# Input projections of two mixing stages: float32 products, or three passes of rounded parts split on chip

## What is computed

```python
def token_mix(x, w_in, w_out, ...):
    h = x @ w_in
    (nq, kc, vc, ks, vs, kw, vw, gl, u, gq, gk, gv, ga, gr) = jnp.split(h, split_pts, axis=-1)
    gates = jax.nn.sigmoid(gl).reshape(B, S, NSA_HEADS, 3)
    o_a = nsa_mixer(nq, kv(kc), kv(vc), kv(ks), kv(vs), kv(kw), kv(vw), gates, ...)
    o_b = pool_mixer(u, pool_w, pool_scale)
    o_c = gla_mixer(gq, gk, gv, ga, gr, gla_wa2, gla_ba, gla_norm_g)
    return jnp.concatenate([o_a, o_b, o_c], axis=-1) @ w_out
```

## Time and profile before

| | |
|---|---|
| median of three runs | 2523.66 us |
| the profiled execution | 2522.78 us |
| its span | 2521.0 us |
| granted TensorE clock, mean | 0.973 |
| stage mix0, first product to first L1485 | 220.1 to 284.8 us |
| stage mix1, first product | 766.5 us |
| last products of mix0 (L1423) | until 366.3 us |

### The profile page before, as it was taken

One profiled execution on the slowest core, in us unless ns is written; L12 is line 12 of the kernel. 1 busy time (PEld: TensorE's weight loads), 2 busy tenths in 40 slices (PEclk: granted clock), 3 DMA queues, 4 the chain that ended last, 5 costly groups with the idle time before them and its releaser, 6 DMA issues.

```text
span 2521.0 us, 32805 instructions
## 1 busy us (share of the span) xinstructions
PE 2393.3 (95%) x12825; PEld 1937.4 (77%) x12825; DVE 1778.3 (71%) x2016; ACT 1259.1 (50%) x1345; POOL 148.5 (6%) x175
## 2 busy tenths in 40 slices
PE   7999999999999999989998997889999999999996
PEld 6878858887878768779846885667788888887885
DVE  5773357858763458758454566868889889899897
ACT  4332334334332434344424436737777777777774
POOL 0000000001000000000010003500000000000000
PEclk9999999999999999999999997889999999999998
DMA  9667248757757358644215553138999999999994
GB/s 324 242 248 183 65 150 274 279 182 268 254 201 170 101 185 282 218 176 167 101 67 197 178 175 110 68 142 289 353 354 355 369 334 359 364 354 345 361 350 190
DMA packets 304844, 591.48 MB, mean 235 GB/s; under 512 B 61583, under 2 KB 97109, under 8 KB 304605
## 3 DMA queue, kind: packets, MB, share of 16 engines
q1 hardware_dynamic: 285954, 521.09, 59.0%
q0 software_dynamic: 18352, 68.70, 8.0%
q10 hardware_dynamic: 428, 0.15, 0.0%
HBM read 587.79 MB, written 2.11 MB: 234 GB/s over the span
## 4 chain that ended last, share of the span: by engine, by line
PE 86%; DVE 8%; ACT 3%; issue 2%; DMA 0%; DVEq 0%; SPq 0%; ACTq 0%
PE psum L891 20%; PE psum L893 19%; PE psum L892 19%; PE psum L1361 3%; PE psum L924 3%; PE psum L1368 2%; PE psum L1423 2%; DVE ring_r L1093 2%; PE psum L2084 2%; PE psum L1014 2%; PE psum L2817 2%; PE psum L1981 1%; PE psum L1986 1%; PE psum L1982 1%; DVE arena L3000 1%
## 5 line engine op out<-in xcount | busy, mean ns | idle before, releaser
L1093 DVE TENSOR_TENSOR ring_r<-ring,ring_r 128x2048 fp32r<-128x2048 f32 x286 | 653.3, 2289 | 261.4 <-ACT ring_r L1087 260.8
L1087 ACT CAST ring_r<-ring 128x2048 fp32r<-128x2048 f32 x286 | 546.1, 1911 | 492.8 <-PE psum L893 403.9
L893 PE MATMUL psum<-ring_r,arena_r 128*128 128x512 f32 (+1 forms) x1560 | 596.9, 383 | 0.0
L891 PE MATMUL psum<-ring_r,arena_r 128*128 128x512 f32 (+1 forms) x1016 | 398.6, 392 | 23.1 <-DVE arena_r L1165 11.1
L892 PE MATMUL psum<-ring_r,arena_r 128*128 128x512 f32 (+1 forms) x1016 | 391.2, 385 | 0.0
L1093 DVE TENSOR_TENSOR ring_r<-ring,tail_r 128x2048 fp32r<-128x2048 f32 x143 | 327.3, 2289 | 83.1 <-ACT tail_r L1087 81.8
L1087 ACT CAST tail_r<-ring 128x2048 fp32r<-128x2048 f32 x143 | 273.3, 1911 | 139.4 <-PE psum L893 137.7
L893 PEld LDWEIGHTS psum<-ring_r,arena_r 128*128 128x128 f32 x1560 | 294.5, 189 | 58.0
L893 PE MATMUL psum<-ring_r,z_r 128*128 128x512 f32 (+1 forms) x840 | 311.2, 370 | 0.0
L891 PEld LDWEIGHTS psum<-ring_r,arena_r 128*128 128x128 f32 x1016 | 192.2, 189 | 75.7 <-DVE ring_r L1093 22.7
L892 PEld LDWEIGHTS psum<-ring_r,arena_r 128*128 128x128 f32 x1016 | 192.6, 190 | 35.1
(11 more groups left out here) (467 smaller groups left out, 3239.3 us busy)
## 6 DMA issues: line engine op xcount, KB each, us to landing
ring<-in_moe_w SPq DMA_DIRECT2D x264, 1024.0 KB, 6.7
arena<-in_ada_w POOLq DMA_DIRECT2D x48, 1024.0 KB, 9.1
ring<-in_ffn_wg SPq DMA_DIRECT2D x44, 1024.0 KB, 7.3
ring<-in_ffn_wu SPq DMA_DIRECT2D x44, 1024.0 KB, 7.1
ring<-in_ffn_wd SPq DMA_DIRECT2D x44, 1024.0 KB, 7.0
ring<-in_ffn_w SPq DMA_DIRECT2D x33, 1024.0 KB, 5.4
ring<-in_mlstm_w_in SPq DMA_DIRECT2D x8, 2048.0 KB, 8.3
ring<-in_mlstm_w_out SPq DMA_DIRECT2D x4, 2048.0 KB, 8.9
```

The source lines that it names most:

```text
L891: pe.matmul(dst, lhs_low, rhs, start=start, stop=False)
L893: return pe.matmul(dst, lhs, rhs_low, start=False, stop=stop)
L1087: act.copy(upper[i % UPPERS], place(PN[r.key, i])).then_inc(upper_ready, 1)
L1093: dve.tensor_tensor(low, raw, upper[i % UPPERS], ALU.subtract).then_inc(lower_ready, 1)
```

## The change

Two tables are new: nine pieces of the panels, and the PE event after which each piece's buffer is free. Every piece is split on chip. `mix_high_act` (ACT) waits for the panels of the piece and for its buffer, and writes the rounded high part to one of three buffers (two in a part of the arena that the attention uses later, one in `tail`). `mix_low_dve` (DVE) waits for that and writes the rest over the raw piece. Ahead of a mixing stage ACT's copies of x go to `xh`, rounded, and `mix_split_x_dve` writes the rest to `xT_r`. `features` and `tokens` wait for the piece's low part and make three float32r passes for each float32 matmul of before; in piece 0 the pass over x's rest waits for it. PE's order is changed, and with it two of the events that free a panel (panel 0: gqk in place of gv, panel 1: ga in place of gr).

```diff
-PANEL_END = ("gv", "gr", "q1", "kcvc", "vwgl", "u")
+PANEL_END = ("gqk", "ga", "q1", "kcvc", "vwgl", "u")
+
+PIECES = [[(0, 256, 256)], [(1, 0, 272)], [(0, 0, 256)], [(2, 0, 256)], [(2, 256, 256)], [(3, 256, 128), (4, 128, 128)],
+          [(3, 0, 256)], [(4, 0, 128), (4, 256, 152)], [(5, 0, 256)]]
+PIECE_END = ("gv", "ga", "gqk", "q0", "q1", "kskw", "kcvc", "vwgl", "u")
...
+    def mix_high_act(act, l, c):
+        for i, first, w in PIECES[c]:
+            act.wait_ge(*landed(PN["mix", l, "in", i]))
+        if c < 2:
+            act.wait_ge(mod_done, (2 * l + 1) * NC)
+        elif c == 2:
+            for b in PN["mix", l, "upper"].before:
+                act.wait_ge(*b)
+        else:
+            act.wait_ge(*mixP.after(PIECE_END[c - 3], l))
+        for high, raw in zip(upper_pieces(c), raw_pieces(l, c)):
+            ins = act.copy(high, raw)
+        ins.then_inc(*mixH.inc(f"hi{c}", l))
+
+    def mix_low_dve(dve, l, c):
+        dve.wait_ge(*mixH.after(f"hi{c}", l))
+        for high, raw, low in zip(upper_pieces(c), raw_pieces(l, c), raw_pieces(l, c, ring_r)):
+            ins = dve.tensor_tensor(low, raw, high, ALU.subtract)
+        ins.then_inc(*mixL.inc(f"lo{c}", l))
...
-        def features(dst, i, first, m):
-            w = IN_PANELS[i][1]
-            pe.wait_ge(*landed(pn[i]))
+        def features(dst, c, j, first, m):
+            pe.wait_ge(*mixL.after(f"lo{c}", l))
...
             for k in range(KD):
-                mm = pe.matmul(dst, panel(pn[i], KD, w)[:, k, first:first + m], xT[:, k, :], start=k == 0, stop=k == KD - 1)
+                pe.matmul(by_tile, high[:, k, cols], xh[:, :, k, :], start=k == 0, stop=False)
+                pe.matmul(by_tile, low[:, k, cols], xh[:, :, k, :], start=False, stop=False)
+                mm = pe.matmul(dst, high[:, k, cols], xT_r[:, k, :], start=False, stop=k == KD - 1)
             return mm
...
+        def tokens(dst, c, j, first, m, t):
+            pe.wait_ge(*mixL.after(f"lo{c}", l))
...
             for k in range(KD):
-                mm = pe.matmul(dst, xT[:, k, t * P:(t + 1) * P], panel(pn[i], KD, w)[:, k, first:first + m],
-                               start=k == 0, stop=k == KD - 1)
+                pe.matmul(dst, xh[:, t, k, :], high[:, k, cols], start=k == 0, stop=False)
+                pe.matmul(dst, xh[:, t, k, :], low[:, k, cols], start=False, stop=False)
+            if c == 0:
+                pe.wait_ge(*mixX.after(f"x{2 * t + 1}", l))
+            for k in range(KD):
+                mm = pe.matmul(dst, xT_r[:, k, t * P:(t + 1) * P], high[:, k, cols], start=False, stop=k == KD - 1)
             return mm
...
+                    for t in range(NT):
+                        mix_high_act(act, int(later[3:]), t)
+                        ln_act(act, m, t)
+                        copy_xT_act(act, m + 1, t)
+                    mix_high_act(act, int(later[3:]), 2)
...
+                    ln_dve(dve, step, m, acc, [(first_tile_done, m + 1), ACC_READY[m]],
+                           lambda: mix_low_dve(dve, l, 0), lambda: mix_split_x_dve(dve, m + 1, 0))
+                    mix_low_dve(dve, l, 1)
+                    mix_split_x_dve(dve, m + 1, 1)
+                    mix_low_dve(dve, l, 2)
```

More of the change, by code:

```diff
@@ L331, in program @@
     six = range(6)
-    mixP = Events(sem("mix_pe"), ["ga", "gqk", "pre", "gv", "gr", "q0", "q1", "kdT", "at", "kskw", "dS", "vs", "vwgl", "kcvc",
+    mixP = Events(sem("mix_pe"), ["gv", "gr", "ga", "gqk", "pre", "q0", "q1", "kdT", "at", "kskw", "dS", "kcvc", "vs", "vwgl",
                                   "gla0", "gla1", "s0", "s1", "cmp1", "t0", "t1", "v0", "s2", "v1", "s3", "cmp2", "sc",
@@ L342, in program @@
                                    "pc_sub", "pT2", "p3", "pc", "m4", "pT3", "p4", "m5", "pT4", "p5", "pT5"])
+    mixH = Events(sem("mix_high"), [f"hi{c}" for c in range(len(PIECES))])
+    mixL = Events(sem("mix_low"), [f"lo{c}" for c in range(len(PIECES))])
+    mixX = Events(sem("mix_x_low"), [f"x{i}" for i in range(4)])
     mixG = Events(sem("mix_pool"), ["zeros", "sr"])
@@ L438, in program @@
             l = int(st[3:])
+            PN["mix", l, "upper"] = rg.take(TAIL, dmas=0, over=mixP.after("u", l))
             for i in range(len(IN_PANELS)):
@@ L1314, in program, with upper_pieces, raw_pieces, mix_split_x_dve @@
     UNITS = [(0, 0, 0, REP), (0, 1, 0, REP)] + [(1, b, r, 2) for b in range(2) for r in (0, 2)]
+    mix_upper = [arena_r[:, pieces_at:pieces_at + HALF], arena_r[:, pieces_at + HALF:pieces_at + HALF + KD * 280], tail_r[:, :]]
+    def upper_pieces(c):
+        at, views = 0, []
+        for i, first, w in PIECES[c]:
+            views.append(mix_upper[c % 3][:, at:at + KD * w].rearrange("p (k w) -> p k w", w=w))
+            at += KD * w
+        return views
+    def raw_pieces(l, c, of=None):
+        views = []
+        for i, first, w in PIECES[c]:
+            slot = (ring if of is None else of)[:, PN["mix", l, "in", i].slot, 0:KD * IN_PANELS[i][1]]
+            views.append(slot.rearrange("p (k w) -> p k w", w=IN_PANELS[i][1])[:, :, first:first + w])
+        return views
+    def mix_high_act(act, l, c):
+        for i, first, w in PIECES[c]:
+            act.wait_ge(*landed(PN["mix", l, "in", i]))
[14 more added lines that the diff above has]
+        ins.then_inc(*mixL.inc(f"lo{c}", l))
+    def mix_split_x_dve(dve, q, t):
+        for b in range(2):
+            i = 2 * t + b
+            part = slice(4 * b, 4 * b + 4), slice(t * P, (t + 1) * P)
+            dve.wait_ge(xT_ready, 4 * q + i + 1)
+            dve.tensor_tensor(xT_r[:, part[0], part[1]], psum[:, i, :].rearrange("p (k n) -> p k n", k=4),
+                              xh[:, t, part[0], :], ALU.subtract).then_inc(*mixX.inc(f"x{i}", MIX_OF[q]))
     def bank(i):
@@ L1459, in mix_pe @@
         pe.wait_ge(*mixA.after("q0", l))
-        features(half(6, 0), 3, 256, P)
-        features(half(6, 1), 4, 128, P).then_inc(*mixP.inc("kskw", l))
+        features(half(6, 0), 5, 0, 0, P)
+        features(half(6, 1), 5, 1, 0, P).then_inc(*mixP.inc("kskw", l))
         pe.wait_ge(*mixA.after("kdT", l))
@@ L1525, in mix_pe @@
         pe.wait_ge(*mixV.after("oC1", l))
-        tokens(half(3, 0), 5, 0, 256, 0)
+        tokens(half(3, 0), 8, 0, 0, 256, 0)
         pe.wait_ge(*mixV.after("vblk", l))
```

57 lines of the change are left out of this document (38 added, 19 removed).

## The result

The changed kernel takes 2534.21 us, the median of 5 runs (2532.23 to 2536.89), against 2523.66 before; the ratio is 1.0042, interval [1.0031, 1.0053]. It is slower. The forecast was 2530.1. The profiled execution is one of 2536.89 us with a span of 2534.9.

The account below looks back on a forecast made before the run. PE, busy 95% of the span, was taken as the bound. Per stage -9.8 + 3.6 + 2.3 + 4.0 + 1.4 + 1.7 = +3.2 us, two stages +6.4, giving 2530.1 us; range 2516 to 2540.

Parts of the forecast that it names:

- 1 wide products: In each mixing stage, 136 products with 256 columns, each 0.072 us shorter as three passes: 9.8 us less.
- 2 narrow products: vs and vwgl, 128 and 152 moving columns: 96 float32r matmuls at 0.120 us, 3.6 us more a stage.
- 3 wait for x's rest: After gv tile 0's high-x passes PE waits for DVE's two subtractions: 2.3 us a stage.
- 4 wait for piece 1: PE waits for piece 1's low part, which stands behind DVE's norm of tile 1: 4.0 us a stage.
- 5 wait for piece 5: PE waits for piece 5: panels 3 and 4 land after gqk, then casts and subtractions: 1.4 us a stage.
- 6 clock at the start: After PE's mostly idle 221.9 to 229.3 us the granted clock falls: 1.7 us a stage, bounds 0 and 3.
- B: Rival: short passes of vs and vwgl cost 0.067 us; with a clock that stays, 2516.5 us, faster; chance 0.07.
- C: Rival: each short pass of vs and vwgl costs a float32 product, 0.247 us: 2554.5 us; chance 0.10.
- Rival D: Panels 3 and 4 need 2.5 us more to land, the wait for piece 5 is 3.9 us: 2535.1 us; chance 0.12.
- Rival A: The clock stays at the stage's start, so 1.7 us a stage fall out: 2526.7 us; chance 0.24.

Follow-up runs that it names:

- wide: Changed kernel with vs and vwgl as 48 float32r passes of 304 columns instead of 96 of 128 and 152: 2523.14 us, ratio to before 1.0001.
- swap: Changed kernel with panel 4 issued ahead of panel 3 on SP's queue: 2529.37 us, ratio to before 1.0022.
- w1early: w1late with ACT taking piece 5 ahead of the Silu of gr, as in swapearly: 2506.07 us, ratio to before 0.9933.
- fill: Changed kernel with five unread float32 products of 512 columns in PE's first two waits of each mixing stage: 2531.58 us, ratio to before 1.0036.
- order: Changed kernel with gqk, which frees panel 3, ahead of gr tile 1 and ga: 2533.57 us, ratio to before 1.0039.
- wideopen: Changed kernel with the edits of wide and open together: 2517.59 us, ratio to before 0.9977.
- w1late: swapopen with the w1 panel, needed only at cmp1, issued behind panels 4 and 3: 2507.02 us, ratio to before 0.9938.
- open: Changed kernel with high passes first at the stage's start, piece 1's low part last, ACT's high part of piece 2 earlier: 2526.29 us, ratio to before 1.001.
- swapopen: wideopen with the issue order of swap: 2516.02 us, ratio to before 0.9976.
- swapearly: swapopen with ACT taking piece 5 ahead of the Silu of gr: 2515.03 us, ratio to before 0.9964.

## Why the prediction was right, and where its sizes were off

The sign and the mechanism held: three passes win the wide products, and short passes, waits for splits and the clock give back more than that. The sum was +3.2 us a stage; +5.4 and +5.1 were measured, so two thirds more. By its steps, for one stage, all from start to start in the timelines:

| step | forecast | mix0 | mix1 | from |
|---|---|---|---|---|
| 1 wide products | -9.8 | -10.4 | -10.4 | 120 products ahead of L1485: 52.5 us, 43.1 as three passes; u 1.0 less |
| 2 narrow products | +3.6 | +3.0 | +3.0 | 10.8 us for 96 passes, less 7.8 |
| 3 wait for x's rest | +2.3 | +2.3 | +2.3 | as forecast |
| 4 wait for piece 1 | +4.0 | +4.0 | +4.0 | 4.92 us with eight passes in them |
| 5 wait for piece 5 | +1.4 | +2.5 | +2.4 | start of `at` to start of kskw, less 0.65 |
| 6 clock at the start | +1.7 | +2.3 | +2.2 | 5.2 and 5.1 us for 24 passes instead of 2.9 |
| clock at cmp1 | 0 | +1.8 | +1.7 | 22.0 and 21.9 us from cmp1 to u instead of 20.2 |
| sum | +3.2 | +5.5 | +5.2 | +5.4 and +5.1 by the stages |

From the first product to the first one of the gated linear attention I expected 69 us; it is 69.4 (221.0 to 290.4) against 64.6. I had also named as a sign of being wrong that the parts outside the stages change their length; they did, by 3.4 us in the profiled execution, no more than they differ among the other traces.

**Step 1** was a little too small: I took the float32 product from one group of 64 records, 0.432 us, and over the 120 products it is 0.437. A pass costs 0.120 us, as forecast. This error and that of step 2 cancel a part of what steps 5 and 6 lacked.

**Step 2** settled the rivals of both signs. A short float32r pass costs 0.112 us, not 0.067 (B) nor 0.247 (C), close to the 0.110 at which short float32 records stand apart; B's sign turned at 0.104 and 0.087, so it was near. The figure of the Trainium skill that I weighed there ("TensorE: Matmul & The Clock Gate", "Wait — 56ns, not 53.3ns?", 55.6 ns from start to start at 128 columns) is half of what this trace shows. Here each pass has 4-byte operands and a weight load of its own; which of the two makes the difference, no run separates, and that the load sets the 0.112 us is my reading. wide then showed that a moving operand of 304 columns in two segments costs 0.143 us, 304 / 2.4 GHz plus 16 ns. So the count of passes, not that of columns, set the price of vs and vwgl.

**Step 5** was mis-sized, by no single error. From the end of gqk to `at` PE took the 13.0 us that I had. Behind gqk I had 14.3 us to the end of the low part (10 for the landing, 4.2 for the splits). It was 15.3 (251.5 to 266.8): the landing 10.4, another half microsecond until ACT began, and 4.4 for the splits. swap shows that the landing counted, and that 1.2 us stay while ACT makes piece 5 behind the scaling of q0; w1early, where it makes it earlier, has no wait. Rival D's mechanism was there, at 0.4 us of landing instead of 2.5.

**Step 6** was mis-sized as well. The clock was low for 10.2 us in mix0 (225.0 to 235.2) and 6.8 in mix1 (781.4 to 788.2), and all but the last of the 24 passes of gr tile 0 fell into it. fill, which keeps the clock up there, gives back 2.0 to 2.5 us a stage. Rival A, a clock that stays, is refuted.

**What the prediction did not have** is the clock at cmp1, a stretch in which the change touches nothing and the clock fell before too. Of the twelve traces it is low for 10.2 us in both stages in seven (before, fill, order, wide, wideopen, w1late, w1early), for 13.7 in both in two (changed, open), and for one each in three, with the same instructions in both stages (swap, swapopen, swapearly). So it can't be put down to the change's instructions there. What makes it long or short no run shows. It is worth 1.7 to 1.8 us in each stage of the changed kernel. Whether the median of the changed kernel carries the whole 3.5 us of it or a part, one trace can't tell.

## What to carry to other kernels

Splitting an operand on chip cost little in engine time here (ACT 34 us and DVE 46 us more busy time in the whole kernel, most of it beside PE's work) and much in order: look at the first product behind every layer norm and at the first piece that comes from a late panel, because there the split stands on the path. Give PE the passes that need only what is there, and make the cast of a piece as soon as its panel lands. Float32r passes of 128 to 256 columns cost nearly the same here, so put narrow products side by side in one moving operand. And before counting on an earlier wait to pay, look at the DMA queue ahead of the panel: here a panel that nobody needed for 45 us stood in front, worth 9 us once the start, the short passes and the issue order were mended, while the two edits meant to bring piece 5 forward (the new issue order, the earlier cast) gave nothing that can be told from noise on top of wideopen.

## What the runs showed that I had not expected

- A wait can cost more than its length. In the changed kernel waits of 2.14 and 3.72 us with 1.2 us of work between them brought 6.8 us at 1.2 GHz in mix1; 2.14 and 2.85 with 2.1 between them brought 10.2 in mix0. A single wait of 2.41 us brought 3.4 us in open, one of 2.48 none in the changed kernel, and 1.22 us none in w1late.
- 128, 152 and, nearly, 256 columns cost the same in a float32r pass: 0.112, 0.112 and 0.120 us; 304 cost 0.143.
- The same low stretch at the same instructions is 10.2 or 13.7 us long, from stage to stage of one execution; by the changed kernel's 1.7 and 1.8 us a stage, this alone moves the kernel by up to 3.5 us.
